# The stage between mixers and feed-forward as interleaved strands, with a layer norm's gain and bias folded into the next modulation

## The chip, the cores and the metric

One NeuronCore of one Trainium2 chip. The metric is the device time of one execution of the whole program in microseconds. All weights come from HBM in float32; matrix products take each float32 operand as a high and a low part and add three products, so each weight tile is copied to its high part by ScalarE (ACT) and its low part is subtracted by VectorE (DVE) before TensorE (PE) uses it. The kernel takes about 3 ms; the change concerns stages of 80 to 160 us.

## The reference

A first block of two layers, then a second block of two attention layers that the change doesn't touch. D = 1024, 256 tokens. One layer of the first block, cut to what matters:

```python
mod = silu(c) @ mod_w[layer] + mod_b[layer]
sh_m, sc_m, gt_m, sh_f, sc_f, gt_f = split(mod, 6)
h = x * (1 + sc_m) + sh_m
u, q, k, v, g_out, a_low = split(h @ w_in[layer], IN_SPLITS)
y_s5 = s5(u, ...)                    # gelu(y) * sigmoid(gelu(y) @ w_glu + b_glu)
y_gla = gated_linear_attention(q, k, v, g_out, a_low, ...)
y = concatenate([y_s5, y_gla]) @ w_out[layer]
x = layer_norm(ALPHA * x + (1 + gt_m) * y, ln_mix_g[layer], ln_mix_b[layer])
h = x * (1 + sc_f) + sh_f
f = swiglu(h) if layer == 0 else moe_swiglu(h)      # 8 experts, top 2
x = layer_norm(ALPHA * x + (1 + gt_f) * f, ln_ffn_g[layer], ln_ffn_b[layer])
```

The layer norm is normalisation, then gain and bias per column, and h after it is again a scale and a shift per column.

## The kernel before

Each engine has its own program, and in-order waits on semaphores tie them together. At stage borders `fence` makes every engine wait for all the others. The stages of layer l of the first block are: w_in (modulate, transpose, project), mixers, out, feed-forward, and a second layer norm. Weights pass through a ring of five 1 MB slots (`RG`): SP issues a load when the low parts of the slot's former tile are made, `W.his` (ACT) writes high parts, `W.los` (DVE) low parts, four parts of 128x1024 (WH, WL) at a time; a part's place is free again when PE has used it.

Inside the start and the mixers, the work of an engine is cut into strands (Python generators), and `weave` runs their pieces in the order of a string in `ORDERS`: each letter is the next piece of a strand (s the S5 mixer, g the gated attention, m the modulation's products, b the preparation of the next S5 weights). The order is fixed when the kernel is built. A piece that waits holds all pieces behind it on its engine.

The out stage is written straight on (`pe_glu`, `v_glu`, `a_glu`, L1505 to 1559). In order: layer 0 makes the first eight of fourteen weight jobs of the next layer's S5 (PE transposes, ACT copies; `JOBS`: eight B, two C, four K); in layer 1 ACT issues the 13 small loads of `a_second_in` instead. Then the H transposes of the attention's output, the glu product (48 matmuls of 256 columns), its tanh on ACT, a product on DVE, the scaled copy on ACT, and its low part on DVE (steps z, e). Then w_out: two column halves of four parts, 96 matmuls of 512 columns, rows 0 to 7 of eight row blocks in order, where rows 0 to 3 hold the S5 mixer's part (yE) and rows 4 to 7 the attention's (gE).

`v_post_ln` (L1577) then waits for all of w_out, and for each token half t adds both column halves to X; ACT sums (`a_post_ln`). In layer 0 DVE runs the last six S5 jobs (C, K) between these adds and the mean. Then mean, squares with sum on ACT, root (with a table load), and per t the normalisation (`ts`), gain and bias on columns 0 to 703 on DVE and on columns 704 to 1023 on POOL (`g_post_ln`). PE waits for all four, transposes X (`pe_h_mod`), DVE scales and shifts with the columns MC (`v_h_mod`), ACT and DVE split, and after a fence the feed-forward begins. The dense feed-forward (`v_ffn`) has seven blocks; beside them DVE adds layer 1's modulation sums (`v_beside`) and next S5 weights (`v_s5_out`). The second layer norm of layer 0 and that of layer 1 use the same `v_post_ln`.

## Time and profile before

| | |
|---|---|
| median of 3 runs | 3031.71 us (3031.06 to 3036.01) |
| the profiled execution, its own time | 3035.59 us |
| its span, first to last instruction | 3033.8 us |
| start, to 131.5 | 131.5 us |
| mixers, layer 0, 131.5 to 293.5 | 162.0 us |
| out, layer 0, 293.5 to 385.8 | 92.3 us |
| dense feed-forward, 385.8 to 653.4 | 267.6 us |
| layer norm and w_in, 653.4 to 733.0 | 79.6 us |
| mixers, layer 1, 733.0 to 866.6 | 133.6 us |
| out, layer 1, 866.6 to 948.7 | 82.1 us |
| router, experts, layer norm, to 2080 | 1131.3 us |
| second block, to the end | 953.8 us |

The span is cut where one stage's first instruction starts. A stage's length less an engine's busy time is that engine's idle time in it; only the waits that end last set the length.

### The profile page before, as it was taken

The page shows a single profiled execution, that of the slowest core. Times are in us where ns is not written, and L with a number is a line of the kernel's source. Part 1 is how long each engine was busy: PE and PEld are TensorE (multiplying, and loading weights), DVE is VectorE, ACT ScalarE, POOL GpSimd, SP SyncE. Part 2 cuts the span into 40 slices and gives each one's busy share as a digit, 9 for nine tenths or more (in the row PEclk, how much of TensorE's full clock was granted, in tenths as well). Part 3 has the DMA queues.
Part 4 walks back from the last instruction along what each step waited for, and adds up shares of the span by engine and source line. Part 5 has one row for each costly group of instructions (what it writes and reads, how often), then busy time and mean ns, then how long its engine had stood idle before and what let it go on. Part 6 is the DMA issues. An engine that isn't in the chain of part 4 may idle for free.

```text
span 3033.8 us, 31530 instructions
## 1 busy us (share of the span) xinstructions
PE 2564.1 (85%) x11717; PEld 2005.6 (66%) x11717; DVE 2055.8 (68%) x2190; ACT 1563.5 (52%) x1922; POOL 41.4 (1%) x45
## 2 busy tenths in 40 slices
PE   5987589969764999999999999995777998886898
PEld 2736577758444777777777777774545786655687
DVE  5686577664745787888888788875664554575454
ACT  2222334333133787787878778764443544544443
POOL 0000000000100000000000000000000000000000
PEclk9986799988776999999999999997777999977899
DMA  8451247642131898989989898983212454303252
GB/s 250 140 186 45 87 161 256 243 169 85 42 126 57 304 361 300 338 332 339 332 312 356 310 346 325 340 332 112 78 42 83 140 189 149 129 14 111 97 181 96
DMA packets 274625, 599.11 MB, mean 197 GB/s; under 512 B 28753, under 2 KB 35215, under 8 KB 273313
## 3 DMA queue, kind: packets, MB, share of 16 engines
q1 hardware_dynamic: 252144, 580.30, 53.8%
q10 hardware_dynamic: 22322, 16.75, 2.0%
q8 instruction: 93, 1.52, 0.2%
q14 instruction: 66, 0.54, 0.1%
HBM read 595.91 MB, written 1.09 MB: 197 GB/s over the span
## 4 chain that ended last, share of the span: by engine, by line
PE 63%; DVE 21%; ACT 10%; issue 2%; ACTq 1%; DMA 1%; POOL 0%; DVEq 0%; POOLq 0%; PEldq 0%
PE PS L205 61%; DVE WL L167 6%; ACT WH L197 3%; PE PS L213 3%; ACT AR L197 2%; DVE AR L167 2%; DVE MW L167 1%; ACTq L146 1%; DVE WF L167 1%; ACT MW L197 1%; DVE HF L167 1%; DVE MOD L167 1%; ACT L197 1%; DVE HTR L167 1%; ACT WF L197 1%
## 5 line engine op out<-in xcount | busy, mean ns | idle before, releaser
L167 DVE TENSOR_TENSOR WL<-RG,WH 128x1024 fp32r<-128x1024 f32 (+1 forms) x558 | 919.2, 1647 | 487.6 <-ACT WH L197 464.4
L197 ACT ACTIVATE WH<-RG 128x1024 fp32r<-128x1024 f32 x782 | 827.4, 1058 | 612.1 <-PE PS L205 542.2
L205 PE MATMUL PS<-WH,HTR 128*128 128x512 f32 (+3 forms) x2920 | 926.8, 393 | 62.1 <-DVE HTR L167 22.8
L205 PEld LDWEIGHTS PS<-WH,HTR 128*128 128x128 f32 x2920 | 557.2, 193 | 198.0 <-DVE WL L167 35.3
L205 PE MATMUL PS<-WL,HTR 128*128 128x512 f32 (+3 forms) x1460 | 568.6, 389 | 0.0
L205 PE MATMUL PS<-WH,ATR 128*128 128x512 f32 x1624 | 520.3, 394 | 12.9 <-DVE ATR L167 7.3
L205 PEld LDWEIGHTS PS<-WH,ATR 128*128 128x128 f32 x1624 | 307.9, 190 | 79.9 <-DVE WL L167 14.4
L205 PE MATMUL PS<-MW,HTR 128*128 128x512 f32 x1332 | 331.0, 398 | 18.1 <-DVE MW L167 18.1
L205 PE MATMUL PS<-WL,ATR 128*128 128x512 f32 x812 | 318.6, 392 | 0.0
L205 PEld LDWEIGHTS PS<-WL,HTR 128*128 128x128 f32 x1460 | 282.9, 194 | 52.9
L167 DVE TENSOR_TENSOR MW<-RG,MW 128x2048 fp32r<-128x2048 f32 x112 | 256.7, 2292 | 63.0 <-ACT MW L197 52.8
L205 PEld LDWEIGHTS PS<-MW,HTR 128*128 128x128 f32 x1332 | 249.3, 190 | 70.6 <-DVE MW L167 20.0
L197 ACT ACTIVATE MW<-RG 128x1024 fp32r<-128x1024 f32 x224 | 237.9, 1062 | 24.9 <-PE PS L205 2.4
L213 PE MATMUL PS<-KC,AR 128*128 128x128 f32 (+2 forms) x716 | 121.5, 309 | 67.5 <-DVE AR L167 28.5
L205 PEld LDWEIGHTS PS<-WL,ATR 128*128 128x128 f32 x812 | 154.1, 190 | 31.2
L213 PEld LDWEIGHTS PS<-KC,AR 128*128 128x128 f32 (+2 forms) x716 | 97.5, 160 | 94.0 <-DVE AR L167 31.4
L213 PE MATMUL PS<-KC,X 128*128 128x128 f32 x160 | 35.0, 409 | 110.1 <-POOL X L167 35.9
L205 PE MATMUL PS<-RG,SMALL 128*1 128x512 f32 x256 | 121.2, 625 | 4.3 <-ACT MOD L197 2.0
L197 ACT ACTIVATE AR<-PS,SMALL 128x128 f32<-128x128 f32 (+3 forms) x146 | 77.5, 531 | 72.7 <-PE PS L205 64.5
L197 ACT ACTIVATE AR<-PS 128x512 f32<-128x512 f32 (+3 forms) x120 | 66.7, 556 | 83.8 <-PE PS L205 54.2
L213 PEld LDWEIGHTS PS<-KC,X 128*128 128x128 f32 x160 | 31.9, 222 | 113.6 <-DVEq L155 59.8
L197 ACT ACTIVATE ATR<-PS 128x512 fp32r<-128x512 f32 x102 | 61.1, 599 | 80.2 <-PE PS L213 75.0
(217 smaller groups left out, 2053.6 us busy)
## 6 DMA issues: line engine op xcount, KB each, us to landing
RG<-in_moe_w_gate SPq DMA_DIRECT2D x112, 1024.0 KB, 5.4
RG<-in_moe_w_up SPq DMA_DIRECT2D x112, 1024.0 KB, 5.6
RG<-in_moe_w_down SPq DMA_DIRECT2D x112, 1024.0 KB, 5.9
RG<-in_w_ff SPq DMA_DIRECT2D x64, 1024.0 KB, 5.2
RG<-in_mod_w SPq DMA_DIRECT2D x48, 1024.0 KB, 5.3
RG<-in_w_in SPq DMA_DIRECT2D x36, 1024.0 KB, 5.2
RG<-in_w_out SPq DMA_DIRECT2D x16, 1024.0 KB, 5.0
RG<-in_ffn_w_gate SPq DMA_DIRECT2D x14, 1024.0 KB, 5.2
```

Source lines behind the costliest of these rows:

```text
L146: return Ins(self.e.dma_start(dst, src, **kw) if self.e is not None else None, self)
L167: return self.did(lambda: self.e.tensor_tensor(o, a, b, op))
L197: return self.did(lambda: self.e.activation(o, a, f, bias=bias, scale=scale))
L205: return self.did(lambda: self.e.matmul(o, l, r, start=start, stop=stop))
L213: return self.did(lambda: self.e.transpose(o, a, perm))
```

## The change

- **The out stages become strands** (`pe_out`, `v_out`, `a_out`): x is the stage's own chain, from the y copy to the modulated H; w are 14 pieces of one high or low part each; r are the S5 jobs (layer 0) or the transposes and copies for the second block (layer 1). Orders `out0` and `out1` are new. In layer 0 the C and K jobs on PE stand behind w_out's last part (r11 to r16), those on DVE among the layer norm's pieces, the last two behind the normalisation.
- **w_out from its lower rows on**: each column half is loaded and multiplied as row blocks 4 to 7, then 0 to 3; only the latter wait for the glu's result.
- **Its halves added apart**: DVE adds column half 0 (both t) as soon as its four parts are used, and ACT sums it, while PE is at half 1; one more tiny add joins the sums.
- **Gain and bias folded**: after three of the four layer norms (r = 0, 1, 2) only the normalisation is done before the transposes. `v_ln_cols` (three operations of 128x8) folds gain and bias into MC. X itself gets them later, in `v_ln_rest` (four operations of 128x1024): for r = 0 two each in dense blocks 1 and 2, for r = 1 behind the projection's evictions, for r = 2 in block 5 of the first four experts (into H). POOL's share is left only at r = 3. The rows for gain and bias are loaded at other places, each after the former rest.
- **Moved besides**: the 13 loads of `a_second_in` and two rows go from the out stage of layer 1 into its mixers, between the second and third of six levels of the attention's second half on ACT (b2, behind g14); four small loads and one transpose and copy are added at the start; one fence of each engine before w_in of layer 1 is gone; the orders of mixers 0 are new on ACT, PE and DVE.

```diff
 ORDERS = {
-    ("mixers0", "a"): "sgmbsbmggmsggmmmmmggggggmsmmsmgggsggggsssggg",
+    ("mixers0", "a"): "gmsbmsbgmgsggmmmmmggggggmsmmsggggsgggsmssggg",
-    ("mixers0", "pe"): "gsmmgmmsmmgmgmggmmggmmmsmssmmggssssggsmsgsgsssgsgssssgsssssggggggggg",
-    ("mixers0", "v"): "gsmbsgbgbggsgsbgbggbggbggbsssggggggggggsmggmgggmgggggsgssgssggggggggggg",
-    ("mixers1", "a"): "sgmbssggggsgggsgggsgggggmgsgssmmggmmg",
+    ("mixers0", "pe"): "mmggsmmsmmmmsmmgsmmgmggmggmsmssggssssggsssggsssggsssgsmssssggggggggg",
+    ("mixers0", "v"): "bggsbgsgbgsmgssssgbbggbggbggbgggggggggsggggggsgggggmgmsggmggsggssgggggg",
+    ("mixers1", "a"): "sgmbssggggsgggsgggsgggbggmgsgssmmggmmg",
...
+    ("out0", "a"): "xxrrwwrxxrrwwwrrwxrrxxwwwwwxwxwwwxxxxxxxx",
+    ("out0", "pe"): "rrrxxrrxrrxrrrxxxxxxxxxrrrrrrxxxx",
+    ("out0", "v"): "xwrxwxxwwwwxxxxwrwwwxwwwwxrrxwrxrxrrxxxxxxxx",
+    ("out1", "a"): "xxwwwwxxwwrrxwxxwwwrwxwxwwwxxxxxxxx",
+    ("out1", "pe"): "xxrxxxxxrxxxxxxxxxx",
+    ("out1", "v"): "xwrxwwwxxwwxxwxxwwrrwxwrwwwxwxxxxxxxxxxx",
...
+        def plan_out(l):
+            for h in range(2):
+                out = []
+                for k0 in (4, 0):
+                    W.plan(("w_out", l, h, k0), w["w_out"][l][k0 * 128:(k0 + 4) * 128, h * 512:(h + 1) * 512], 4, 512)
...
+        def v_ln_cols(v, l, gain, bias, isc):
+            c = 48 * l + 8 * isc
+            s, b = MC[:, c:c + 8], MC[:, c - 8:c]
+            v.tt(sm(304, 8), LNC[:, bias:bias + 8], s, MUL)
+            v.tt(b, b, sm(304, 8), ADD)
+            return v.tt(s, s, LNC[:, gain:gain + 8], MUL)
...
         def a_mixers(a, l):
             weave(a, f"mixers{l}", s=a_s5(a, l), g=a_gla(a, l), m=a_mods(a, l),
-                  b=iter(()) if l else once(lambda: a_s5_in(a, 1)))
+                  b=once(lambda: (a_second_in(a), a_ln_rows(a, 1, "mix", 1))) if l else once(lambda: a_s5_in(a, 1)))
...
+            for h in range(2):
+                for p in W.of["w_out", l, h]:
+                    yield
+                    pe.wait_ge(W.lo, p.los)
+                    if p.k0 < 4:
+                        pe.wait_ge(glu_v, l, f"e{p.k0}")
...
+        def v_post_ln(v, r, gt, parts, acc=None):
+            for h in range(2):
+                c = slice(h * 512, (h + 1) * 512)
+                if acc is None:
+                    yield
+                    v.wait_ge(W.used, parts[h].i + 1)
+                for t in range(2):
+                    if acc is None:
+                        v.tt(H[:, t, c], PS[:, 2 * t + h, :], gt[:, c], MUL)
+                        v.stt(X[:, t, c], X[:, t, c], ALPHA, H[:, t, c], MUL, ADD).then_inc(ln_v, f"x{h}{t}")
...
             for t in range(2):
                 v.ts(X[:, t], X[:, t], S_LN[:, t:t + 1], SS_LN[:, t:t + 1], ADD, MUL).then_inc(ln_v, f"n{t}")
-                v.tt(X[:, t, 0:704], X[:, t, 0:704], gain[:, 0:704], MUL)
-                x = v.tt(X[:, t, 0:704], X[:, t, 0:704], bias[:, 0:704], ADD)
+                if acc is not None:
+                    v.wait_ge(ln_in, 2 * r + 2)
...
+        def v_ln_rest(v, r, to):
+            v.wait_ge(ln_in, 2 * r + 2)
+            for t in range(2):
+                v.tt(to[:, t], X[:, t], GAIN, MUL)
+                yield
+                x = v.tt(to[:, t], to[:, t], BIAS_LN, ADD)
...
+        def pe_out(pe, l):
+            def x():
+                yield from pe_glu(pe, l)
+                def ready():
+                    if l == 0:
+                        pe.wait_ge(sw_v, 1, "jobK3")
+                    else:
+                        pe.wait_ge(rt_v, 0, "bias")
+                    pe.wait_ge(ln_v, 2 * l, "n1")
+                yield from pe_h_mod(pe, 2 * l + 1, ready)
+            def jobs():
+                yield from pe_s5_jobs(pe, 1, (2, 3), JOBS[:8])
+                yield
+                pe.wait_ge(glu_a, 0, "t2")
+                yield from pe_s5_jobs(pe, 1, (4, 5, 6, 7), JOBS[8:])
+            weave(pe, f"out{l}", x=x(), r=once(lambda: pe_second_in(pe)) if l else jobs())
+        def v_out(v, l):
+            def x():
+                yield from v_glu(v, l)
+                yield from v_post_ln(v, 2 * l, GTM, [W.of["w_out", l, h][-1] for h in range(2)])
+                yield from v_h_mod(v, 2 * l + 1, l, 4)
+            def los():
+                for _ in range(14):
+                    yield
+                    W.los(v, 1)
...
-        def v_beside(v, n):
+        def v_beside(v, n, rest):
+            if n in (1, 2):
+                run(rest, 2)
+            if n == 5:
+                v.wait_ge(sums_a, 1)
+                v_ln_cols(v, 1, 32, 40, 1)
             for i in SUMS_BY[n]:
                 v_sums(v, i)
...
         def pe_w_in(pe, l):
-            yield from pe_h_mod(pe, 2 * l)
+            yield from pe_h_mod(pe, 2 * l, lambda: pe.wait_ge(ln_v, 1, "n1") if l else None)
...
         def v_w_in(v, l):
             yield from v_h_mod(v, 2 * l, l, 1)
-            yield from v_project(v, ("w_in", l), INC1, PR1, AHEAD1)
+            rest = v_ln_rest(v, 1, X) if l else None
+            yield from v_project(v, ("w_in", l), INC1, PR1, AHEAD1, (lambda j: run(rest, 1)) if l else (lambda j: None))
...
+            for at, n, src in ((0, 16, w["ln_mix_g"]), (16, 16, w["ln_mix_b"]), (32, 8, w["ln_ffn_g"][0:1]), (40, 8, w["ln_ffn_b"][0:1])):
+                a.dma(CB[at:at + n, 256:384], src.rearrange("l (j p) -> (l j) p", p=128)).then_inc(first_in)
...
-                    v_moe(v, W, moe_pe, moe_v, moe_a, 0)
+                    rest = v_ln_rest(v, 2, H)
+                    v_moe(v, W, moe_pe, moe_v, moe_a, 0, lambda e, n: run(rest, 1) if n == 5 else None)
...
-                    a_moe(a, W, moe_pe, moe_v, moe_a)
+                    a_moe(a, W, moe_pe, moe_v, moe_a, lambda e, n: a_ln_rows(a, 1, "ffn", 2) if (e, n) == (4, 5) else None)
```

## Rows read from the trace of the kernel before

**Rows 1.** Page, part 1: busy time by engine, share of the span, instructions.

```profile
PE 2564.1 (85%) x11717; PEld 2005.6 (66%) x11717; DVE 2055.8 (68%) x2190; ACT 1563.5 (52%) x1922; POOL 41.4 (1%) x45
```

**Rows 2.** Windows by stage: length, busy us of PE, PEld, DVE, ACT, POOL; clock; DMA share; GB/s.

```profile
131.50:293.50 162.00, 134.85 (x703) 75.36 (x703) 130.27 (x198) 32.13 (x49) 8.74 (x12) 0.77 0.38 121
293.50:385.80 92.30, 52.50 (x273) 46.90 (x273) 50.94 (x68) 34.72 (x45) 5.80 (x4) 0.76 0.27 91
...
733.00:866.60 133.60, 104.37 (x648) 65.72 (x648) 90.46 (x134) 29.79 (x45) 9.12 (x12) 0.77 0.19 64
866.60:948.70 82.10, 38.62 (x171) 31.73 (x171) 44.69 (x57) 30.21 (x38) 5.80 (x4) 0.71 0.30 104
948.70:2080.00 1131.30, 1032.97 (x4659) 838.18 (x4660) 920.66 (x591) 842.51 (x904) 5.83 (x4) 0.97 0.85 312
```

**Rows 3.** Chain that ended last: start us, us, what.

```profile
305.05 5.76 PE PS L205 x48
...
317.78 23.94 PE PS L205 x96
...
351.57 9.51 PE PS L205 x64
...
376.55 1.10 PE PS L213 x4
...
570.39 32.67 PE PS L205 x144
```

**Rows 4.** DVE timeline, out 0: start us, us, instruction, [idle before <-releaser].

```profile
344.88 0.69 DVE L175 SCALAR_TENSOR_TENSOR X<-X,H 128x512 f32<-128x512 f32 x1
...
350.03 1.49 DVE L171 TENSOR_SCALAR AR<-PS 128x512 f32<-128x512 f32 x2
...
362.04 1.51 DVE L175 SCALAR_TENSOR_TENSOR MOD<-KC,SMALL,MOD 128x128 f32<-128x128 f32 x4
...
368.83 0.81 DVE L172 TENSOR_SCALAR X<-X,SMALL 128x1024 f32<-128x1024 f32 x1
```

**Rows 5.** ACT timeline, out 0.

```profile
299.16 5.42 ACT L197 ACTIVATE AR<-PS 128x512 f32<-128x512 f32 x8
...
311.92 1.99 ACT L197 ACTIVATE AR<-PS,SMALL 128x256 f32<-128x256 f32 x4
...
363.86 1.15 ACT L198 ACTIVATE H<-X,SMALL 128x1024 f32<-128x1024 f32 x1 [12.75 <-DVE SMALL L171]
...
366.45 1.28 ACT L197 ACT_TABLE_LOAD   x1
```

**Rows 6.** ACT timeline, out 1; ACTq is the issue of a DMA.

```profile
871.10 0.60 ACTq L146 DMA_DIRECT2D AR<-in_moe_b_router  x1
...
872.90 4.38 ACT L197 ACTIVATE WH<-RG 128x1024 fp32r<-128x1024 f32 x4
```

**Rows 7.** PE timeline, out 1.

```profile
880.87 0.76 PE L205 MATMUL PS<-HTR,WH 128*128 128x256 f32 x2 [12.34 <-DVE HTR L175]
...
939.50 3.65 PE L213 MATMUL PS<-KC,X 128*128 128x128 f32 x16 [20.37 <-POOL X L167]
```

**Rows 8.** DVE timeline, dense FFN.

```profile
437.45 3.88 DVE L167 TENSOR_TENSOR WL<-RG,WH 128x1024 fp32r<-128x1024 f32 x3
...
467.75 9.73 DVE L175 SCALAR_TENSOR_TENSOR H<-RG,SMALL,H 128x2048 f32<-128x2048 f32 x4
```

**Rows 9.** PE timeline, dense FFN.

```profile
478.86 0.79 PE L205 MATMUL PS<-WH,ATR 128*128 128x512 f32 x1 [3.91 <-DVE WL L167]
```

**Rows 10.** ACT timeline, mixers 1.

```profile
818.15 0.95 ACT L197 ACTIVATE WF<-WF 128x256 f32<-128x256 f32 x2
820.67 0.42 ACT L197 ACTIVATE WF<-WF 128x256 f32<-128x256 f32 x1 [1.57 <-DVE WF L167]
```

**Rows 11.** DVE timeline, mixers 0.

```profile
224.51 1.28 DVE L167 TENSOR_TENSOR MOD<-PS,KC 128x512 f32<-128x512 f32 x2 [3.46 <-PE PS L205]
...
280.67 1.66 DVE L178 TENSOR_REDUCE WF<-MOD 128x128 f32<-128x896 f32 x1
```

More of the change, by code:

```diff
@@ L490, in build @@
         SUMS_BY = (), (0,), (1, 2), (3,), (4, 5), (6,), (7,)
+        def plan_out(l):
[3 more added lines that the diff above has]
+                    W.plan(("w_out", l, h, k0), w["w_out"][l][k0 * 128:(k0 + 4) * 128, h * 512:(h + 1) * 512], 4, 512)
+                    for p in W.of.pop(("w_out", l, h, k0)):
+                        p.k0 += k0
+                        out.append(p)
+                W.of["w_out", l, h] = out
         plan_mod(0, 0, 4)
@@ L1435, in v_mods @@
             v_cols(v, 1 + l)
+            v_ln_cols(v, l, 8 * l, 16 + 8 * l, 4)
             if l == 0:
@@ L1574, in build @@
         ln_v, ln_a, ln_g = signal("ln_v"), signal("ln_a"), signal("ln_g")
-        S_LN, SS_LN = sm(8, 2), sm(12, 2)
-        def v_post_ln(v, r, gt, gain, bias, acc, between=nothing):
-            for t in range(2):
-                for h in range(2):
-                    c = slice(h * 512, (h + 1) * 512)
-                    v.tt(H[:, t, c], PS[:, 2 * t + h, :] if acc is None else acc[:, t, c], gt[:, c], MUL)
-                    x = v.stt(X[:, t, c], X[:, t, c], ALPHA, H[:, t, c], MUL, ADD)
-                x.then_inc(ln_v, f"x{t}")
-            between()
+        S_LN, S_LN2, SS_LN = sm(8, 2), sm(10, 2), sm(12, 2)
@@ L1606, in a_post_ln, with a_ln_rows @@
             x.then_inc(ln_a, "square")
+            yield
             a.wait_ge(ln_v, r, "var")
             a_root(a, 0, 2).then_inc(ln_a, "root")
-        def g_post_ln(g, r, gain, bias):
-            g.wait_ge(rows_in, ROWS_LN[r])
+        SCR_LN = H
+        def a_ln_rows(a, l, name, after):
+            if after is not None:
+                a.wait_ge(ln_v, after, "rest")
+            for at, x in ((GAIN, "g"), (BIAS_LN, "b")):
+                a.dma(at, rowb(w[f"ln_{name}_{x}"][l, :])).then_inc(ln_in)
@@ new lines, in v_out, with jobs @@
+        def v_out(v, l):
[5 more added lines that the diff above has]
+                for _ in range(14):
+                    yield
+                    W.los(v, 1)
+            def jobs():
+                yield
+                v.wait_ge(glu_v, 0, "e2")
+                v_s5_cx(v, 1)
+                yield from v_s5_jobs(v, 1, (4, 5, 6, 7), JOBS[8:])
+            weave(v, f"out{l}", x=x(), w=los(), r=v_second_in(v) if l else jobs())
@@ L1618, in build, with a_out, x, his @@
+        def a_out(a, l):
+            def x():
+                yield from a_glu(a, l)
+                yield from a_post_ln(a, 2 * l)
+                yield from a_h_mod(a, 2 * l + 1)
+            def his():
+                for _ in range(14):
+                    yield
+                    W.his(a, 1)
+            weave(a, f"out{l}", x=x(), w=his(), r=a_second_out(a) if l else a_s5_jobs(a, 1, (2, 3), JOBS[:8]))
         SG = AR[:, 2048:3072].rearrange("p (t n) -> p t n", t=2)
@@ L1751, in v_second_in @@
         def v_second_in(v):
+            yield
             v.wait_ge(rt_pe, 0, "gains")
@@ L1921, in pe_moe, with v_moe @@
             scatter(NE - 1)
-        def v_moe(v, P, s_pe, s_v, s_a, part):
+        def v_moe(v, P, s_pe, s_v, s_a, part, beside=nothing):
             slots = KC[:, K_IOTA + 128 * part:K_IOTA + 128 * part + 128]
@@ L1967, in v_moe @@
                 P.los(v, 4)
+                beside(e, n)
                 if n == 0 and e:
@@ L1977, in v_moe, with a_moe @@
             scatter(NE - 1)
-        def a_moe(a, P, s_pe, s_v, s_a):
+        def a_moe(a, P, s_pe, s_v, s_a, beside=nothing):
             def gather(e):
@@ L2024, in a_moe @@
                 P.his(a, 4)
+                beside(e, n)
                 if n == 0 and e:
@@ L2938, in pe_program @@
                 if l:
-                    pe.fence(ends)
                     run(pe_w_in(pe, 1))
@@ L2943, in pe_program @@
                 pe.fence(ends)
[L2944 to L2953 removed]
+                pe_out(pe, l)
                 pe.fence(ends)
@@ L2990, in v_program @@
                 if l:
-                    v.fence(ends)
                     run(v_w_in(v, 1))
@@ L3047, in a_program @@
                 if l:
-                    a.fence(ends)
                     run(a_w_in(a, 1))
@@ L3101, in g_program @@
             for l in range(L):
-                if l:
-                    g.fence(ends)
                 g.fence(ends)
```

157 lines of the change are left out of this document (83 added, 74 removed).

## Prediction

> **What bounds the kernel now.** I read the page's busy times first: PE is busy for 85% of the span, DVE 68%, ACT 52%, POOL 1% [rows 1]. That hides that the stages differ, so I cut the span into stages [rows 2]. The experts take 1131.3 us with PE busy for 1033.0 of them, at clock 0.97 and a DMA share of 0.85: nothing there is to be had from the order of small steps. The out stages are the opposite: in 92.3 us PE works 52.5, in 82.1 us it works 38.6, at a mean clock of 0.76 and 0.71, with no other engine near full and DMA at 0.27 and 0.30. They are chains of waits. The chain itself says where: in layer 0 the glu product, w_out's 96 matmuls in 23.94 us to 341.72, and the transposes at 376.55, that is 34.8 us later, in which it did only the K products [rows 3]. In layer 1 PE had been idle 12.34 us when the glu began at 880.87, and 20.37 us when the transposes began at 939.50, the last wait ending with POOL [rows 7]. So the question is how much of these waits the new order takes out, and what the moved work costs where it lands.
>
> **Out, layer 0 (old: 24.3 us to w_out, 24.0 in it, 34.8 to the transposes, 9.2 to the feed-forward).** Before w_out PE has 8 jobs, the H transposes and the glu. A job's four transposes I take as 0.92 us, the H transposes as 1.8; both are estimates from the stretch's PE busy time. An ACT copy of a job is 0.68 (5.42 for 8) [rows 5], and it now runs between PE pieces. PE to the tanh: six jobs 5.5 + 1.8 + glu 5.76 [rows 3] = 13.1; the last two jobs lie beside the tanh of 1.99 [rows 5], for which PE's job strand waits (r10 stands in front of w_out). With a short wait that makes 15 at most and 14.2 if later jobs run at the higher level; I take 14.7: w_out starts at 308.2, 9.6 earlier. Its lower rows need only gE; z and e (two DVE steps and an ACT copy of 1.1, together about 4 us) lie beside two parts of 5.4 us. w_out itself: 96 matmuls at 32.67/144 = 0.227 us [rows 3] are 21.8, where the old ones took 23.9 because PE began them after a wait, at the lower of its levels (1.2, not 2.4 GHz). It ends at 330.0. Half 0's adds and sums are hidden beside half 1.
>
> After it: half 1's adds, 4 x 0.72 from 0.69 [rows 4], 2.9; two C evictions 1.49 [rows 4]; they stand in front of the mean, whose ACT copy (0.85) they cover: 334.5. From here two chains run. The K products take PE 9.51 us [rows 3] from 334.5 to 344.0, the last eviction 0.7: 344.8. The layer norm: mean 0.4, two squares with their reads 2.5, table load 1.28 and root 0.2 [rows 5], root's four small operations 0.9, two `ts` of 0.82 [rows 3], some small gaps and two K evictions in the way: 342.5. So the K jobs end last; PE's transposes wait for K3 (the wait in `ready`), to 344.9. What is late next is DVE: behind K3 stand its four 128x128 steps, 1.51 [rows 4], and a small one, so modulation starts at 346.6 and takes 8.1 as before (9.2 from the transposes' start at 376.55 to the stage's end at 385.8, less 1.1 [rows 2, 3]): the feed-forward starts at 354.7 instead of 385.8. **Gain 31.1.** What goes: ACT's squares had waited 12.75 us for a mean that stood behind six jobs [rows 5], and 376.55 - 368.83 = 7.7 us between the first `ts` and the transposes become 1.65 [rows 3]. Bounds: 34 if no K eviction delays anything, 26 if the eight job copies (5.4 us) all land on the chain.
>
> **Out, layer 1.** ACT issued 13 loads before anything else; the last issue ended at 871.70 [rows 6], 5.1 us after the fence at 866.6. Now y (1.06), one high part (4.38/4 = 1.09) [rows 6] and one low part (1.3) stand before the glu: 870.3, not 880.87. The glu takes 7.8 (5.76 and some 2 for a start at the lower level), w_out follows at once, with `pe_second_in` inside (1.8, an estimate) and 21.8 of matmuls, to 901.7. Before, PE came to an end 20.37 ahead of 939.50, at 919.1 [rows 7]. Then adds 2.9, a half's sum 0.85, mean 0.4, squares 2.5, table and root 1.5, 0.9, two `ts` 1.65, gaps 0.7: 913.1, not 939.50 [rows 7]. **Gain 26.4.** The low parts for the experts end just where half 1 does, as before, and cost nothing more. Bounds 21 and 28.
>
> **Layer norm after the dense feed-forward**: the same 7.7 becomes 1.65, the last half-row sum saves 0.4 and the added tiny add costs 0.2: **gain 6.2**, bounds 5.8 and 6.5. The rest for r = 1 (4 x 1.27) falls on DVE while it idles 1.5 us in each 2.72 us part: nothing; uncovered it would be 5.
>
> **What the moved work costs.** Dense blocks 1 and 2: two operations of 128x1024 each, a third of 3.88, 1.27 with its gap [rows 8]. In block 1 the low parts come up 1.8 us before PE wants them (an estimate from the cadence of the parts), so 2.5 leaves 0.7. In block 2 PE already waits 3.91 for DVE [rows 9], behind 9.73 us of sums [rows 8], and the loads of w_down wait for the same sums; all 2.5 lands. **Loss 3.2**, bounds 0 and 5.
>
> Mixers 1: the 15 DMA issues (13 at 5.12 in all, two more at the same 0.4) are 6.0 us on ACT, which isn't fenced off there. Before: two exponentials at 818.15, the next at 820.67, after 1.57 us of waiting for DVE [rows 10]. The issues start at 819.1 and end at 825.2; DVE's level chain, PE's scores behind it, and the modulation row that PE's next products wait for all move by 3.4. The new `v_ln_cols` (3 x 0.2) stands between the two last products of the attention's gate: 0.6. **Loss 4.0**, bounds 0.6 and 6.6.
>
> Here the Trainium skill speaks otherwise: DMA: Bandwidth & Descriptors, section Issuing engines are not separate DMA queues, says that the sequencer time to initiate a DMA is usually small beside the DMA. In the trace 13 issues held ACT for 5.1 us. By the rule the mixers would lose 0.6 and out 1 gain 5.1 less, and the sum be -55.8; by the rows it is the -57.5 below.
>
> Mixers 0: DVE is busy for 130.3 of 162.0 [rows 2]. I laid the new orders over the timeline. DVE's long S5 step moves ahead of four weight pieces and PE's modulation products fill its shadow; the attention's scores then start where they did. In the rounds DVE waits 3.46 us for PE, since S5 pieces of PE stand between scores [rows 11]; there are two fewer now, and the S5 evictions leave the start of the second half, whose last reduction ended at 282.3 [rows 11]: **gain 3**, bounds 8 and a loss of 4.
>
> Start: four more small issues of about 0.45 on ACT in front of the S5 loads, one transpose, one copy, a wait for seven loads instead of three. The queue had been full there, so most is absorbed: **loss 1**, bounds 0 and 2.5. Experts: DVE is busy 920.7 of 1131.3 [rows 2]; four operations of 1.27 and 1 MB of rows: **loss 1**, bounds 0 and 3. The last layer norm and the second block: 0.
>
> Another rule against the change: VectorE: DVE Perf Modes, section on the TRN2 errata, has a fixed latency per instruction that a large tile pays once. The rows agree: a copy of 512 took 0.68, one of 1,024 1.09 [rows 5, 6]; four half sums instead of two wholes cost 0.5, but all but the last lie beside PE.
>
> **The sum**: -31.1 - 26.4 - 6.2 - 3 + 3.2 + 4.0 + 1 + 1 = -57.5. The profiled execution's own time was 3035.59 (span 3033.8), so it would become 2978.1; it lay 3.9 above the median of 3031.71, and from the median it is 2974.2. I predict **2975**.
>
> **Rivals.**
> - *The strands hold each other up.* Every order is in-order; w_out waits behind r10, modulation behind K3. If the job pieces cost what they did before (C, K: 12.5 us instead of some 4) and one more wait of 4 us appears in each out stage, 17 of the 57.5 go: 2991. For it: every stage so far is far from full, and a missed wait always costs. Against: few job pieces stand in front of x pieces that matter.
> - *The moved pieces are free.* ACT idles much in mixers 1 (29.8 busy of 133.6 [rows 2]); if issues don't hold the exponentials and mixers 0 gain 8: -9, 2966.
> - *The halves don't come early since weights don't.* w_out's parts need ring slots; if loads end last, PE waits in both out stages. DMA shares of 0.27 and 0.30 [rows 2] speak against. It would take 12 us of each: 2999.
> - *Slower.* In mixers 0 PE holds eight of sixteen halves of modulation products (28 us) and all its attention pieces behind s3, which waits for DVE's long S5 step. If that step came late by D, the stage grows by D. All 28 plus four weight pieces of 17 make +45, with the bounds' 31.7 left of the gain: 3045. It decides at D = 31.7 then, and at 60 with the other terms as forecast. The sixteen halves fit in my tracing, so little speaks for it.
>
> **Chances and range.** Forecast 0.60, held strands 0.17, free pieces 0.13, late weights 0.06, slower 0.04. The bounds of all terms add to -76 and -32; most independent, so the range is 2961 to 2994, which reaches both near rivals. About 0.2% (6 us) is what the measurement tells from no change: faster 0.94, same 0.02, slower 0.04.
>
> **What would show it.** Out 0 about 61 us long and out 1 about 56; w_out in 22 us right behind the glu in layer 1; the K products as the last wait before the transposes in layer 0; no POOL before the last layer norm; the wait of 3.91 in block 2 grown to 6.4; ACTq issues between two exponentials in mixers 1 with DVE waiting some 3 us. I am wrong if mixers 0 changes by over 8 us, if PE waits for weights in an out stage, or if the experts take over 3 us more.

## The result, and the profile after

The changed kernel took 2990.5 us (median of 4 runs, 2986.8 to 2995.6), the kernel before in the same group 3033.9 (4 runs). The ratio is 0.9855, 95% interval 0.983 to 0.9881: 1.45% faster. From the median of before (3031.7) to the forecast of 2975 were 56.7 us; measured are 43.4.

The span line and part 1 of the changed kernel's page, against [rows 1]:

```profile
span 2985.1 us, 31552 instructions
...
PE 2556.5 (86%) x11718; PEld 1997.7 (67%) x11718; DVE 2058.9 (69%) x2204; ACT 1566.1 (52%) x1938; POOL 24.4 (1%) x33
```

The engines are busy for as long as they were, within 8 us; only POOL has 12 instructions fewer, those of three layer norms. The span is 48.7 us shorter, so nearly all of this is waiting time. The windows by stage (columns as in [rows 2]) say which:

```profile
133.26:289.14 155.88, 132.58 (x703) 72.77 (x704) 131.29 (x201) 32.16 (x49) 8.87 (x12) 0.80 0.40 125
289.14:353.60 64.46, 47.77 (x272) 42.20 (x272) 46.14 (x65) 35.38 (x49) 0.00 (x0) 0.90 0.34 115
694.52:831.76 137.24, 100.60 (x648) 61.97 (x648) 90.83 (x137) 29.78 (x45) 9.35 (x12) 0.77 0.22 70
831.76:887.72 55.96, 37.15 (x171) 31.37 (x171) 40.01 (x54) 31.03 (x42) 0.00 (x0) 0.80 0.40 132
919.22:1982.11 1062.89, 1004.89 (x4527) 812.41 (x4527) 892.26 (x520) 823.03 (x872) 0.00 (x0) 0.99 0.90 329
```

I set the borders of both traces at the same instructions and took a second profile of the kernel before (experiment 9). In us:

| stage | before, two profiles | after | difference to the first | forecast |
|---|---|---|---|---|
| start and mixers 0 | 293.5, 293.5 | 289.1 | -4.4 | -2 |
| out 0 | 92.3, 92.2 | 64.5 | -27.8 | -31.1 |
| dense feed-forward | 254.1, 250.9 | 253.9 | -0.2 | +3.2 |
| last part, layer norm, to w_in | 40.0, 40.0 | 33.6 | -6.4 | -6.2 |
| w_in | 53.2, 53.5 | 53.4 | +0.2 | 0 |
| mixers 1 | 133.5, 133.3 | 137.2 | +3.8 | +4.0 |
| out 1 | 82.2, 82.0 | 56.0 | -26.2 | -26.4 |
| router, experts, last layer norm | 1136.8, 1142.9 | 1144.6 | +7.8 | +1 |
| second block | 948.3, 948.8 | 952.8 | +4.5 | 0 |

The differences add to -48.7, 8.8 short of the -57.5 that the prediction's sum has. The medians are 43.4 apart, another 5.3 less, and that is in the executions chosen: the first profile of before lay 1.7 above the median of this group, the profiled run of the changed kernel 3.6 below its own.

**Out 0.** The PE timeline of the changed kernel:

```profile
305.12 0.47 PE L205 MATMUL PS<-WH,HTR 128*128 128x512 f32 x1 [3.19 <-ACT AR L197]
...
306.69 1.05 PE L205 MATMUL PS<-WH,HTR 128*128 128x512 f32 x2
...
310.00 0.62 PE L205 MATMUL PS<-WH,HTR 128*128 128x512 f32 x2
...
333.33 8.98 PE L205 MATMUL PS<-AR 128*128 128x128 f32 x64 [3.68 <-DVE AR L171]
343.68 1.97 PE L213 MATMUL PS<-KC,X 128*128 128x128 f32 x16 [1.36 <-DVE MOD L167]
353.60 0.80 PE L205 MATMUL PS<-WH,HTR 128*128 128x512 f32 x1 [7.96 <-POOLq L155]
```

w_out starts 16.0 us after the stage's start. It waited 3.19 for ACT: not for the tanh, which ended at 303.5, but for the last two job copies, which stand behind it in ACT's order and ended at 304.9. Behind this wait PE was at its lower level, as it was in the kernel before: two products take 1.05 at 306.7 and 0.62 at 310.0, and w_out takes 23.67, near the 23.94 of [rows 3]. From its end at 328.8 to the feed-forward at 353.6 is 24.8 (24.7 foreseen), with the K products starting 4.6 behind w_out (4.5 foreseen). The DVE timeline of the same stretch:

```profile
337.00 0.69 DVE L167 TENSOR_TENSOR MOD<-PS,KC 128x512 f32<-128x512 f32 x1 [1.92 <-PE PS L205]
...
340.37 1.66 DVE L172 TENSOR_SCALAR X<-X,SMALL 128x1024 f32<-128x1024 f32 x2
342.13 1.49 DVE L167 TENSOR_TENSOR MOD<-PS,KC 128x512 f32<-128x512 f32 x2
...
343.86 1.52 DVE L175 SCALAR_TENSOR_TENSOR MOD<-KC,SMALL,MOD 128x128 f32<-128x128 f32 x4
```

X is normalized at 342.0, K2 and K3 are evicted until 343.6, and 0.06 later the transposes start: the last wait is K3, as forecast. What is late next is also there: K3's four small steps, 1.52 in all, in front of the modulation. In the kernel before, the mean itself stood behind all six jobs [rows 4, 5].

**Out 1.** PE timeline:

```profile
835.68 0.79 PE L205 MATMUL PS<-HTR,WH 128*128 128x256 f32 x2 [1.95 <-DVE WL L167]
...
844.22 0.40 PE L205 MATMUL PS<-WH,HTR 128*128 128x512 f32 x1
...
866.83 0.39 PE L205 MATMUL PS<-WH,HTR 128*128 128x512 f32 x1
878.48 3.65 PE L213 MATMUL PS<-KC,X 128*128 128x128 f32 x16 [11.26 <-DVE X L172]
```

Against [rows 7]: the wait of 12.34 before the glu is 1.95, w_out follows the glu without one, and the 20.37 before the transposes, released by POOL, are 11.26, released by DVE. Measured from the stage's start, the glu begins at 3.9 (3.7 foreseen), w_out ends at 35.5 (35.1), the transposes begin at 46.7 (46.5).

**What the moved work did.** ACT's timeline in mixers 1, where [rows 10] had 1.57 us between the exponentials:

```profile
779.01 0.95 ACT L197 ACTIVATE WF<-WF 128x256 f32<-128x256 f32 x2
779.99 0.33 ACTq L146 DMA_DIRECT2D SMALL<-in_rel_bias  x1
...
785.78 0.45 ACTq L146 DMA_DIRECT2D ROWS<-in_ln_mix_b  x1
786.33 0.95 ACT L197 ACTIVATE WF<-WF 128x256 f32<-128x256 f32 x2 [6.38 <-issue]
```

15 issues stand between two pairs of exponentials, ACT has 6.38 us between them, and DVE's next level waits for it; so do PE's products behind a row that ACT copies after the exponentials:

```profile
786.78 4.28 DVE L167 TENSOR_TENSOR WF<-WF 128x256 f32<-128x256 f32 x7 [4.12 <-ACT WF L197]
```

```profile
788.01 4.88 PE L205 MATMUL PS<-RG,SMALL 128*1 128x512 f32 x8 [5.19 <-ACT ROWS L197]
```

The Trainium skill (DMA: Bandwidth & Descriptors, section Issuing engines are not separate DMA queues) calls an issue's sequencer time usually small beside the DMA. What counted here was what stood behind the issue on ACT: by that rule mixers 1 would have lost 0.6 us, and they lost 3.8. In the dense feed-forward, PE's wait of 3.91 [rows 9] is 6.43 (6.4 foreseen):

```profile
449.85 0.79 PE L205 MATMUL PS<-WH,ATR 128*128 128x512 f32 x1 [6.43 <-DVE WL L167]
```

### The profile page after: what moved, and what is told of

Same layout as the page of the kernel before. It is cut to its first block, busy times and chain, and to the rows that moved or that the text cites. A ratio compares the mean times of both kernels' runs of the same rounds, so it can differ in the third digit from the quotient of the medians.

```text
span 2985.1 us, 31552 instructions
## 1 busy us (share of the span) xinstructions
PE 2556.5 (86%) x11718; PEld 1997.7 (67%) x11718; DVE 2058.9 (69%) x2204; ACT 1566.1 (52%) x1938; POOL 24.4 (1%) x33
## 4 chain that ended last, share of the span: by engine, by line
PE 61%; DVE 23%; ACT 10%; issue 2%; ACTq 1%; DMA 1%; DVEq 0%; POOL 0%; POOLq 0%; PEldq 0%
PE PS L205 59%; DVE WL L167 8%; ACT WH L197 3%; PE PS L213 2%; ACT AR L197 2%; DVE AR L167 2%; DVE MW L167 2%; ACTq L146 1%; DVE WF L167 1%; ACT MW L197 1%; DVE HF L167 1%; DVE MOD L167 1%; ACT L197 1%; ACT WF L197 1%; DVE HTR L167 1%
## 5 line engine op out<-in xcount | busy, mean ns | idle before, releaser
L205 PE MATMUL PS<-WH,HTR 128*128 128x512 f32 (+3 forms) x2920 | 926.2, 393 | 63.2 <-DVE HTR L167 21.9
L167 DVE TENSOR_TENSOR MW<-RG,MW 128x2048 fp32r<-128x2048 f32 x112 | 256.7, 2292 | 64.1 <-ACT MW L197 53.4
L205 PEld LDWEIGHTS PS<-WL,ATR 128*128 128x128 f32 x812 | 154.8, 191 | 31.5
L197 ACT ACTIVATE AR<-PS 128x512 f32<-128x512 f32 (+3 forms) x120 | 66.7, 556 | 82.2 <-PE PS L205 50.0
L213 PE MATMUL PS<-KC,X 128*128 128x128 f32 x160 | 33.8, 393 | 81.1 <-ACTq L155 31.1
```

Source lines behind the costliest of these rows:

```text
L167: return self.did(lambda: self.e.tensor_tensor(o, a, b, op))
L197: return self.did(lambda: self.e.activation(o, a, f, bias=bias, scale=scale))
L205: return self.did(lambda: self.e.matmul(o, l, r, start=start, stop=stop))
L213: return self.did(lambda: self.e.transpose(o, a, perm))
```

## The experiments

Twelve runs were made; where nothing else is said, an edit is made to the changed kernel. Executions of one kernel differ by up to 13 us here, so most readings are lengths of stages in their traces. In the profiles whose edit leaves out 0 alone it took 64.4 to 64.6, once 65.9; out 1 took 54.5 to 56.0. Ratios are to the kernel before in the same group of runs.

**1. The changed kernel again.**

> The changed kernel once more, with nothing edited. In its first profile the experts (first expert matmul to the start of the last layer norm's wait) took 1062.9 us instead of 1055.6, and the second block 952.8 instead of 948.3. Theory A (these 7.3 and 4.5 us are the change's own cost): they come again within 1 us, 1062 to 1064 and 952 to 954. Theory B (they are how one execution differs from another): the experts come out anywhere from 1055 to 1070 and the second block from 947 to 954, and not together. In both cases the stages before the experts repeat within 1 us: out 0 at 64.5, out 1 at 56.0, mixers 1 at 137.2, mixers 0 at 155.9.

Ratio 0.9862 (0.9847 to 0.9877). Out 0 64.5, out 1 55.4, mixers 1 137.9. From the first expert product to the second block 1116.4 (1113.1 in the first profile, 1105.5 before), second block 950.8. Both move by 2 to 3 us between executions and stay above the first profile of before.

**2. The operations for the experts in the router stage.**

```diff
                     v_router(v)
-                    rest = v_ln_rest(v, 2, H)
-                    v_moe(v, W, moe_pe, moe_v, moe_a, 0, lambda e, n: run(rest, 1) if n == 5 else None)
+                    run(v_ln_rest(v, 2, H))
+                    v_moe(v, W, moe_pe, moe_v, moe_a, 0)
```

> The four operations of DVE on 128x1024 (5.1 us in all) that complete X for the residual are done right behind the router's last operation instead of one each in block 5 of experts 0 to 3. There DVE idles for 8.7 us before the first low part of the gathered rows, so the router stage stays at 31.5 us. Theory A (each of the four lands in full, since DVE's low parts set the pace of the experts): the first four experts get shorter by 4 to 5 us together, against the changed kernel in this same group of runs. Theory B (DVE has room beside the loads; the 7.3 us come from the loads of that execution): no difference beyond 1 us, 0 being what I had forecast less 1.

Ratio 0.9849 (0.9835 to 0.9862). The router stage grew from 31.5 to 36.6, which I had not foreseen. DVE's timeline shows why:

```profile
917.49 1.23 DVE L167 TENSOR_TENSOR H<-H,ROWS 128x1024 f32<-128x1024 f32 x1
918.75 0.61 DVE L171 TENSOR_SCALAR AR<-KC,SMALL 128x128 f32<-128x128 f32 x2
...
928.01 1.49 DVE L167 TENSOR_TENSOR HTR<-AR,HTR 128x512 fp32r<-128x512 f32 x2 [8.65 <-ACT HTR L197]
```

The idle 8.65 us lie behind the choice of expert 0 (the 0.61 at 918.75), for which PE waits; I had put 5.1 us in front of it. From the choice of expert 1 to that of expert 3 took 266.7 instead of 270.1 (after) and 271.7 (experiment 1), but the kernel before, which has no such operation there, took 268.8 and 272.8, so this length decides nothing. PE's own waits do. In block 5 of the first four experts it waits in the changed kernel behind the added operation, here for the first time:

```profile
1034.93 0.50 PE L205 MATMUL PS<-WH,HTR 128*128 128x512 f32 x1 [0.81 <-DVE WL L167]
```

The four such waits are 0.81, 0.75, 0.81 and 0.72. The kernel before and this run have none of them. Laid product against product, PE falls behind the kernel before by 3.6 us in all at these four places. So theory A holds in sign, at 3.6 of its 5.1 us.

**3. The loads earlier in mixers 1.**

```diff
-    ("mixers1", "a"): "sgmbssggggsgggsgggsgggbggmgsgssmmggmmg",
+    ("mixers1", "a"): "sgmbssggggsgggsgggsbgggggmgsgssmmggmmg",
```

> In layer 1's mixers ACT issues the 15 loads for router, norms and layer norm rows four pieces earlier, before it waits 16.7 us for the attention's first half, instead of between two pairs of exponentials. Theory (issues hold ACT, and behind it DVE's level chain): mixers 1 go from 137.2 to 133.8 us, and the rest stays. Rival (the 3.8 us that mixers 1 lost come from the layer norm columns and from PE's clock): 136.5 to 137.5.

Mixers 1 took 133.1, as long as before the change. DVE's level chain no longer waits 4.12 us behind the issues:

```profile
776.96 7.73 DVE L167 TENSOR_TENSOR WF<-WF 128x256 f32<-128x256 f32 x13 [1.07 <-ACT WF L197]
```

PE's wait of 5.19 is 1.56, as it was 1.57 in the second profile of before. The ratio, 0.9853 (0.9834 to 0.9871), can't tell 4 us. Theory confirmed: the issues were the loss, 3.6 us by this wait.

**4. Blocks 0 and 1 in place of 1 and 2.**

```diff
-            if n in (1, 2):
+            if n in (0, 1):
                 run(rest, 2)
```

> In the dense feed-forward two of the four operations that complete X go from block 2 to block 0. Theory (blocks 3 and 4 are paced by the loads, which gave back what block 2 lost): PE's wait in block 2 falls from 6.4 to about 3.9, its wait for weights in block 4 grows by the same 2.5, and the stage stays at 253.9 within 0.5. Rival (the 2.5 us are a real loss and something else gained as much): the stage falls to about 251.4.

The wait in block 2 fell to the old value:

```profile
450.14 0.79 PE L205 MATMUL PS<-WH,ATR 128*128 128x512 f32 x1 [3.91 <-DVE WL L167]
```

The stage fell from 253.9 to 251.8, and from block 2 to block 4 it took 63.2, in the changed kernel 63.1. My theory fell: the loads gave nothing back. The rival holds; what "gained as much" was no gain, as experiment 9 shows. Ratio 0.9858 (0.9843 to 0.9873).

**5. The old orders in mixers 0** (the three strings of the kernel before for `a`, `pe` and `v`).

> The changed kernel with the three old orders of layer 0's mixers (each strand has the same number of pieces in both). Start and mixers 0 together took 293.5 us before and 289.1 to 290.2 in four profiles of the changed kernel. Theory (the new orders gain some 5 us of DVE waiting for PE): the mixers' end goes back to 293 to 296, out 0 stays at 64.5. Rival (the gain is PE's clock, or the start): it stays at 289 to 290.5.

Ratio 0.9847 (0.9828 to 0.9866). The mixers ended at 289.4, and out 0 took 64.5: with the new orders they ended at 286.6 to 292.8, so these gained nothing that can be told. Windows of this kernel (columns as in [rows 2]):

```profile
225.00:235.00 10.00, 10.00 (x64) 8.52 (x62) 7.16 (x12) 0.59 (x1) 0.00 (x0) 0.84 0.34 106
235.00:245.00 10.00, 9.48 (x72) 8.10 (x72) 9.00 (x13) 1.05 (x2) 0.00 (x0) 1.00 0.28 106
```

and of the kernel before, second profile (the first has 0.50 and 0.58):

```profile
225.00:235.00 10.00, 10.00 (x42) 8.34 (x40) 5.64 (x7) 0.59 (x1) 0.00 (x0) 0.50 0.33 106
235.00:245.00 10.00, 10.00 (x49) 8.75 (x48) 5.59 (x8) 0.59 (x1) 0.00 (x0) 0.59 0.03 5
```

PE is busy nearly throughout in both and did 136 products in one, 91 in the other. The same 14 products stand in both timelines, at the lower level in the kernel before and at the higher in this one:

```profile
228.01 3.35 PE L205 MATMUL PS<-WF 64*128 64x128 f32 x14
```

```profile
228.28 1.82 PE L205 MATMUL PS<-WF 64*128 64x128 f32 x14
```

With one and the same order, PE's clock rose to 2.4 GHz at about 228 instead of 243. At 243 this kernel is 6.6 us ahead; later waits give 2.5 of them back, and 4.1 are left at the mixers' end. That is the gain in mixers 0.

**6. w_out's upper rows first.**

```diff
-                for k0 in (4, 0):
+                for k0 in (0, 4):
...
-                                       p.l3[:, k, :], kk == 4, kk == 3)
+                                       p.l3[:, k, :], kk == 0, kk == 7)
```

> w_out's rows 0 to 511 come first again in both out stages, so its first products wait for the gate's result e instead of for the glu product; all else as changed. In out 0 the last e came at 308.7 where w_out had begun at 305.1, in out 1 at 851.6 against 849.9. Theory (the row order takes a wait of this length out): out 0 64.5 + 3.6 = 68.1, out 1 56.0 + 1.7 = 57.7, with up to 2 us more each where PE falls to its lower level in the longer wait. Rival (the wait is hidden anyhow, since the last parts end the stage): neither changes by over 1 us.

Ratio 0.9877 (0.9856 to 0.9899). Out 0 took 67.7, out 1 62.2. PE's timeline, w_out's first product in each:

```profile
304.87 0.76 PE L205 MATMUL PS<-WH,HTR 128*128 128x512 f32 x1 [5.50 <-DVE HTR L175]
...
849.40 0.76 PE L205 MATMUL PS<-WH,HTR 128*128 128x512 f32 x1 [5.85 <-DVE HTR L175]
```

In out 0 the wait is 2.3 longer, and w_out takes 24.54 instead of 23.67, since PE's lower level lasts longer; in out 1 the wait is all new (the expectation put w_out's start in out 1 at 849.9; it was at 844.2). The row order is worth 3.2 and 6.3 us.

**7. The halves' adds together.** In `out0` and `out1`, the adds and sums of half 0 stand behind the last weight piece.

```diff
-    ("out0", "a"): "xxrrwwrxxrrwwwrrwxrrxxwwwwwxwxwwwxxxxxxxx",
+    ("out0", "a"): "xxrrwwrxxrrwwwrrwxrrxxwwwwwwwwwxxxxxxxxxx",
...
-    ("out0", "v"): "xwrxwxxwwwwxxxxwrwwwxwwwwxrrxwrxrxrrxxxxxxxx",
-    ("out1", "a"): "xxwwwwxxwwrrxwxxwwwrwxwxwwwxxxxxxxx",
+    ("out0", "v"): "xwrxwxxwwwwxxxxwrwwwwwwwxxrrxwrxrxrrxxxxxxxx",
+    ("out1", "a"): "xxwwwwxxwwrrxwxxwwwrwwwwwxxxxxxxxxx",
...
-    ("out1", "v"): "xwrxwwwxxwwxxwxxwwrrwxwrwwwxwxxxxxxxxxxx",
+    ("out1", "v"): "xwrxwwwxxwwxxwxxwwrrwwrwwwxxwxxxxxxxxxxx",
```

> The adds of w_out's first half and their two sums stand behind all weight pieces, right in front of the second half's, in both out stages. Theory (they are then on the chain): 4 operations of 0.69 more on DVE behind w_out, 2.9 us, of which nothing is hidden in out 1; in layer 0 they move the C evictions too: out 0 64.5 + 2.9 = 67.4, out 1 56.0 + 2.9 = 58.9, plus up to 0.8 for ACT's sums. Rival (PE's K products, 9 us, set the end in out 0 and give room): out 0 within 1 us, out 1 as the theory.

Out 0 67.5 (67.4 foreseen), out 1 57.6 (58.9). In out 1 the low parts for the experts, which had waited behind half 0's adds, moved up 1.4 us, so the adds themselves began earlier. Ratio 0.9854 (0.9835 to 0.9874). The Trainium skill's fixed latency per instruction (VectorE: DVE Perf Modes, section on the TRN2 errata) is there in the rows, with 0.69 for 512 columns and 1.23 for 1,024, so half the width takes more than half the time; but the overlap is worth more than it costs.

**8. K in front of the mean.**

```diff
-    ("out0", "v"): "xwrxwxxwwwwxxxxwrwwwxwwwwxrrxwrxrxrrxxxxxxxx",
+    ("out0", "v"): "xwrxwxxwwwwxxxxwrwwwxwwwwxwrrrrrrxxxxxxxxxxx",
```

> In out 0 DVE does the K evictions and their four small steps in front of the layer norm's mean, as before the change; all else as changed. K3 was evicted at 343.6 and its steps ended at 345.4; mean, two squares, table load and root, rsqrt and the two normalizing operations took 342.0 - 333.4 = 8.6 with two K evictions between. Theory (the interleaving is what out 0 gained most from): the transposes start at about 345.4 + 8.0 = 353.4 instead of 343.7 and the stage goes from 64.5 to 64.5 + 9.7 - 1.7 = 72.5 (the four small steps are then out of the way of the modulation). Rival (other waits fill the time): under 69.

Out 0 took 74.5, 10.1 more where I had expected 8.0; no other edit made a stage so much longer. DVE's timeline:

```profile
345.56 1.51 DVE L175 SCALAR_TENSOR_TENSOR MOD<-KC,SMALL,MOD 128x128 f32<-128x128 f32 x4
...
350.12 0.17 DVE L172 TENSOR_SCALAR ST<-SMALL 128x2 f32<-128x2 f32 x1 [2.58 <-ACT H L198]
```

The whole layer norm now follows the jobs. Ratio 0.987 (0.985 to 0.9891).

**9. The kernel before again.**

> The kernel before, unchanged, for a second profile of it. Its ratio should hold 1. Open are four places where the first profile of before and those of the changed kernel differ in stages that the change hardly touches: the end of mixers 0 (293.5 against 286.6 to 289.9, with the old orders too), the wait for loads in block 4 of the dense feed-forward (block 2 to block 4 took 66.5 against 63.1, but 66.2 and 66.5 in two of the changed ones), the experts (from the first choice to the last 864.2 against 868.2 to 876.0) and the second block (948.3 against 950.3 to 955.2). Theory A (they come from the change): 293 to 294, 66.5, 864 to 865, 948 to 949 again. Theory B (they are how executions differ): some of them fall into the changed kernel's ranges.

Ratio 0.9994 (0.9985 to 1.0003). Mixers 0 ended at 293.5 again, so theory A holds for them. From block 2 to block 4 took 63.3: theory B. ACT's wait in front of block 4's third high part was 8.47 in the first profile and here

```profile
537.84 1.06 ACT L197 ACTIVATE WH<-RG 128x1024 fp32r<-128x1024 f32 x1 [5.30 <-PE PS L205]
```

I took it for a wait for loads. The row names PE, and PE is what differs: ACT waits for a place that PE has to use first, and PE was at its lower level in the first profile and not in this one. The windows of the same 9 us, first profile, then this one:

```profile
532.00:541.00 9.00, 9.00 (x40) 8.00 (x40) 1.22 (x1) 0.59 (x1) 0.00 (x0) 0.62 0.36 124
```

```profile
532.00:541.00 9.00, 8.53 (x51) 7.19 (x50) 2.45 (x2) 2.04 (x3) 0.00 (x0) 1.00 0.37 123
```

The choices of experts 0 and 7 were 868.3 apart (864.2 in the first), just inside the changed kernel's range: theory B. The second block took 948.8: theory A.

**10. Three edits together**: experiments 3 and 4, and the operations for the experts behind the choice.

```diff
             choose(0)
+            first()
             gather(0)
...
-                    v_moe(v, W, moe_pe, moe_v, moe_a, 0, lambda e, n: run(rest, 1) if n == 5 else None)
+                    v_moe(v, W, moe_pe, moe_v, moe_a, 0, first=lambda: run(rest))
```

> Three edits in one: the loads of layer 1's mixers four pieces earlier, two of the four operations in the dense feed-forward from block 2 to block 0, and the four operations for the experts between the choice of expert 0 and its gather, where DVE idles 8.7 us. Behind the router's last operation but in front of that choice they had cost their full 5.1. Theory (each term by its own run, and the idle time covers 5.1 now): mixers 1 -4.1, feed-forward -2.1, experts -4 against the changed kernel, router 31.5: some 10 us less, ratio to before about 0.9825. Rival (the experts' bumps of 1.2 to 2.6 us come anyway): -6.5, about 0.984.

Ratio 0.9827 (0.9813 to 0.984), 2982.6 us: what the theory said, but the interval reaches the rival's 0.984. DVE's timeline at the router:

```profile
906.26 0.61 DVE L171 TENSOR_SCALAR AR<-KC,SMALL 128x128 f32<-128x128 f32 x2
...
910.75 1.22 DVE L167 TENSOR_TENSOR H<-H,ROWS 128x1024 f32<-128x1024 f32 x1
915.40 1.49 DVE L167 TENSOR_TENSOR HTR<-AR,HTR 128x512 fp32r<-128x512 f32 x2 [3.42 <-ACT HTR L197]
```

The idle 8.7 us are 3.4, the router stage is 31.3, and the four waits in the experts are gone: now the operations cost nothing. The feed-forward to block 2 took 93.6 instead of 96.2, but the stage as a whole 254.1, since PE's lower level lasted longer in blocks 2 and 4. Mixers 1 took 135.0: PE's wait of 5.19 is 1.57 again, and 1.9 us go where PE is at its lower level 96 to 98 us into the stage, which it was not in experiment 3. So the stages did not give what the sum has for them, though the total did.

**11. K3 off the chain.**

```diff
-    ("out0", "pe"): "rrrxxrrxrrxrrrxxxxxxxxxrrrrrrxxxx",
-    ("out0", "v"): "xwrxwxxwwwwxxxxwrwwwxwwwwxrrxwrxrxrrxxxxxxxx",
+    ("out0", "pe"): "rrrxxrrxrrxrrrxxxxxxxxxrrrrrxxxxr",
+    ("out0", "v"): "xwrxwxxwwwwxxxxwrwwwxwwwwxrrxwxrxrrxxxxxxxxr",
...
-                        pe.wait_ge(sw_v, 1, "jobK3")
+                        pe.wait_ge(sw_v, 1, "jobK1")
...
-                yield from pe_s5_jobs(pe, 1, (4, 5, 6, 7), JOBS[8:])
+                yield from pe_s5_jobs(pe, 1, (0, 1, 4, 5, 6, 7), JOBS[8:])
```

> As the combined kernel, and in out 0 the K products of channels 2 and 3 go to two banks that the adds have left, the transposes wait for K1 alone, K3's product follows the transposes on PE and its eviction the modulation on DVE, the root's operation stands in front of K0, and K3's small steps move to block 3 of the feed-forward. Theory (K3 set the start of the transposes): they start at 46.9 + 5.3 = 52.0 us of the stage instead of 54.5, and the stage ends 2.4 earlier, 62.1 instead of 64.5. Rival (DVE is then the chain: 8.1 of modulation and the K evictions follow each other whatever the order): 63.8 or more.

The PE timeline:

```profile
333.58 7.19 PE L205 MATMUL PS<-AR 128*128 128x128 f32 x48 [3.68 <-DVE AR L171]
341.45 1.96 PE L213 MATMUL PS<-KC,X 128*128 128x128 f32 x16 [0.69 <-DVE MOD L167]
351.22 0.80 PE L205 MATMUL PS<-WH,HTR 128*128 128x512 f32 x1 [6.01 <-POOLq L155]
```

Transposes at 52.1 of the stage, its end at 61.8 (52.0 and 62.1 foreseen). The stretch from the last part to w_in took 35.2 instead of 33.6, all of it at its first products, where PE is at its lower level in this profile, and block 3 carries K3's steps. Little is left: 0.9818 (0.9802 to 0.9834), 2982.2 us, not to be told from experiment 10. Both beat both kernels: their ten executions took 2975.0 to 2986.7, eight of the changed kernel 2986.3 to 2995.6.

**12. The fold undone in out 0 alone.**

```diff
-            v_ln_cols(v, l, 8 * l, 16 + 8 * l, 4)
+            if l:
+                v_ln_cols(v, l, 8 * l, 16 + 8 * l, 4)
...
                 yield from v_post_ln(v, 2 * l, GTM, [W.of["w_out", l, h][-1] for h in range(2)])
+                if l == 0:
+                    run(v_ln_rest(v, 0, X))
...
-            if n in (1, 2):
-                run(rest, 2)
```

> The fold alone undone, in out 0 alone: DVE multiplies by the gain and adds the bias (four operations of 128x1024, 5.1 us) right behind the two that normalize, the transposes wait for them, and neither the columns in mixers 0 nor the four operations in blocks 1 and 2 of the feed-forward are there. Theory (DVE is the chain there, PE's K products ended only 0.3 us behind the normalizing): the transposes start 5.0 us later in the stage, 59.5 instead of 54.5, out 0 takes 69.5, and the feed-forward gives 3.2 back (blocks 0 to 2 from 96.2 to 93.1), so that the whole is 1.5 to 2 us slower than the changed kernel. Rival (PE's lower level and the K evictions leave room): out 0 under 68, the whole faster than the changed kernel.

The DVE timeline, then PE's:

```profile
340.02 5.01 DVE L167 TENSOR_TENSOR X<-X,ROWS 128x1024 f32<-128x1024 f32 x4
```

```profile
346.68 3.68 PE L213 MATMUL PS<-KC,X 128*128 128x128 f32 x16 [6.47 <-DVE MOD L167]
```

Out 0 took 69.7 (69.5 foreseen), blocks 0 to 2 92.1 instead of 96.2. So in layer 0 the fold took 5.2 us off one chain and paid 4.1 of them on the next. Ratio 0.986 (0.9837 to 0.9882), no different from the changed kernel.

## Why the prediction was right, and where it was off

**The mechanism** was right: the out stages were chains of waits, and their shortening is more than the whole gain. The prices of the parts, each undone alone: K in front of the mean 10.1; the row order 3.2 and 6.3; the halves apart 3.0 and 1.6; the fold in out 0 5.2 before its payment. They overlap with one another, so they are no sum. In out 1 most of the gain was not undone alone: PE's wait in front of the glu fell from 12.34 to 1.95, where the loads had stood, and its wait in front of the transposes from 20.37 to 11.26, of which experiment 7 shows 1.6; the rest is argued from the rows.

**The number** owes something to luck. 2990.5 lies 15.5 above the forecast and 3.5 inside the end of the range. Against the first profile of before, the two stages for which +1 and 0 had been forecast took 11.3 more than that, out 0 gave 3.3 less, and 5.8 of this were hidden by the dense feed-forward and mixers 0, for reasons that the prediction doesn't have.

**Out 0, -27.8 for -31.1**: a size. The term that failed is "w_out starts at 308.2" and "21.8" long. It started 16.0 after the stage's start, not 14.7, because I let the last two job copies lie beside the tanh; in ACT's order they stand behind it. And I gave w_out the higher level although a wait stood in front of it, as before; it took 23.7. These 1.3 and 1.9 make 3.2 of the 3.3. All behind w_out came out within 0.1. (The `ts` that the prediction cites from [rows 3] stands in [rows 4].)

**Out 1, -26.2 for -26.4**, and **the layer norm, -6.4 for -6.2**: as worked out. From the first normalizing `ts` to the transposes it is 634.69 - 632.97 = 1.7 us in the layer norm's trace.

**Dense feed-forward.** The +3.2 is real: from its start to block 2 it took 96.2 instead of 93.1, and against the second profile of before the stage lost 3.0. Against the first it seems to have lost nothing, since in that one PE was at its lower level for longer in block 4 (granted clock 0.62 instead of 1.00 in the 9 us shown in experiment 9), which costs the 3.2 us. I first took this for loads that gave something back; experiments 4 and 9 refuted it.

**Mixers 1, +3.8 for +4.0**: the issues, shown by experiment 3, where PE's wait behind them fell by 3.6 and the stage by 4.1. With other edits beside it, the same move took the same 3.6 out of the wait and 2.2 to 2.4 out of the stage; in experiment 10 the rest went to PE's lower level.

**Mixers 0**: -4.4 with the start, for -2. The size is near, the reason was wrong. I gave it to DVE waiting less for PE; with the old orders it is the same. It is PE's clock, which rises to the higher level 15 us sooner in experiment 5 (the window of 225 to 245 us shows it in the first profile of the changed kernel too, 0.71 and 1.00). Over twelve profiles of changed kernels the mixers ended at 286.6 to 292.8, on average at 289.1, in both of before at 293.5. The start ended at 132.9 instead of 131.2, but at 129.0 to 134.2 in the others, so that its +1 can't be told. What lets the clock rise sooner stays open: from 221 to 228 PE did the same 30 products in the same time in both.

**Experts, +7.8 with router and layer norm for +1.** The prediction's own sign of being wrong, over 3 us more in the experts, came: from the first expert product to the last layer norm's wait they took 1062.9 instead of 1055.6. The failed step is the estimate that four operations on an engine with 19% idle time would be mostly hidden. They cost 3.6 of their 5.1 us, as the four new waits of PE show (experiment 2): DVE's average share hid that its low parts come in rows without a gap. The lengths agree. From the choice of expert 0 to that of expert 7, nine profiles with the operations took 870.9 to 876.0 (mean 872.8), three without 868.2 to 870.1 (868.8), two of before 864.2 and 868.3 (866.3). The rest is not the change's: PE waits 1.4 to 1.8 us for a low part at most once in an expert, at three places in the first profile of before, six in the second and five in the changed kernel, and its lower level behind other waits comes and goes as well. Against the second profile of before the whole row of the table is +1.7.

**Second block, +4.5 for 0.** Not foreseen and not settled. Twelve profiles of changed kernels took 950.4 to 955.2, two of before 948.3 and 948.8. A stretch of its second layer in the first profile after:

```profile
2514.36:2802.50 288.14, 221.33 (x946) 169.41 (x946) 164.13 (x292) 131.30 (x231) 0.00 (x0) 0.80 0.24 78
```

and in the second of before:

```profile
2567.30:2853.20 285.90, 218.83 (x947) 167.14 (x948) 164.65 (x294) 131.93 (x232) 0.00 (x0) 0.82 0.24 79
```

The same products take 2.5 us more of PE at a clock of 0.80 instead of 0.82, while DVE and ACT do the same. It fits PE's level falling and rising elsewhere. Over the whole block, product against product, about 2.8 of the 4.0 us against this profile are products that take longer, the rest small differences in waits. No run here changed the level alone, and why all twelve should lie above both of before is open.

**The rivals.** *Strands hold each other up* came nearest in time (2991), and in kind it happened once: w_out waited for two job copies, 1.3 us beyond the forecast. Its price of 17 us did not come: no new wait of 4 us in either stage, and all behind w_out as forecast. *The moved pieces are free* is refuted by experiments 2 to 4. *Weights late*: no wait for a load in an out stage. *Slower*: mixers 0 did not grow.

## What to carry to other kernels

Work taken off a chain is worth what it costs where it lands: look there for a stretch in which the engine idles and nothing queued behind it is waited for. Four operations cost 5.1 us in front of one small instruction, 3.6 spread over a busy stage, and nothing behind that instruction. An engine's average share doesn't say so, the timeline does; and a few DMA issues are a piece of work on the engine that issues them. Before a difference in an untouched stage is explained, take a second profile of the kernel before, and compare PE's granted clock in that stretch: a wait that names PE may only say that PE was slower.
